# Token sums of the second and third seven-product group on GpSimd instead of VectorE

## The chip, the cores and the metric

One core of a Trainium2 chip runs the whole program in one launch. The metric is the device time of that launch in microseconds (us); lower is better. Engine names in the profile: PE is TensorE (PEld its weight loads), DVE is VectorE, ACT is ScalarE, POOL is GpSimd, SP is SyncE, which only issues transfers here.

## The reference

One decoder layer over 256 tokens of width 2048, all in float32: half a SwiGLU feed-forward, two token mixers side by side, half a second SwiGLU feed-forward, and a final norm.

```python
def rmsnorm(x, g):
    y = xf * lax.rsqrt(jnp.mean(xf * xf, axis=-1, keepdims=True) + NORM_EPS)
    return y * g

def swiglu(x, w_gate, w_up, w_down):
    return (jax.nn.silu(x @ w_gate) * (x @ w_up)) @ w_down

x = x + 0.5 * swiglu(rmsnorm(x, ffn1_norm), ffn1_w_gate, ffn1_w_up, ffn1_w_down)
... dilated attention and forgetting attention on rmsnorm(x, mix_norm) @ w_in, gated, projected, added ...
x = x + 0.5 * swiglu(rmsnorm(x, ffn2_norm), ffn2_w_gate, ffn2_w_up, ffn2_w_down)
return rmsnorm(x, final_norm)
```

D_MODEL is 2048 and D_FF is 5632. The change touches only the two feed-forwards.

## The kernel before

**Precision by splitting.** Each float32 operand of a product is split in two parts: ScalarE rounds it (`w_hi`, `xT_hi`, `pair_hi`), VectorE subtracts the rounded part from the original (`w_lo`, `xT_lo`, `pair_lo`), and TensorE adds three products, hi by hi, hi by lo and lo by hi (lines 551 to 553, 564 to 566). Weights come in slabs of two row tiles by 512 columns. A slab is loaded by SyncE, rounded by ScalarE, split by VectorE, and then used by TensorE. In a feed-forward six slab buffers are in rotation (four called `w_hi`/`w_lo`, two called `more_hi`/`more_lo`), so ScalarE and VectorE can be up to six slabs ahead of TensorE.

**A feed-forward.** D_FF is taken in 11 chunks of 512 columns. The first chunk is computed plainly: 16 slabs (8 of the gate weights, 8 of the up weights), 12 matmuls each. The other ten are "steps" of 33 slabs. Within a step, three of the four groups of row tiles are computed with seven products in place of eight, in Strassen's manner (`paired`). This needs sums of weights, made by VectorE for each step (`weight_sum`, lines 1329 to 1341, tile `sums`), and sums of tokens, made once for each feed-forward and each of the three groups: S1 to S4 in `pair_sums`, rounded by ScalarE into `pair_hi` and split by VectorE into `pair_lo`.

**Making the token sums.** `sum_pairs(f, g)` makes the four sums of group `g` of feed-forward `f` from the scaled, transposed tokens, which lie in `hidden` or `partial` (lines 1363 to 1366, 128 partitions by 256 elements each). S2 reads S1, and S4 reads S2. Then `round_pairs` on ScalarE (line 1006) and `split_pairs` on VectorE (line 1372) work on all four at once. There is one buffer `pair_sums`, so group `g` can be made only once group `g - 1` has been split (semaphore `s_lo`).

**Order around the change.** Every engine's order is written out by hand. During the first 16 slabs, with `o` the slab that TensorE is at, VectorE runs: split of slab `o + 6`, then at `o` = 3, 5, 7 `split_pairs` of groups 0, 1, 2, and at `o` = 4, 6 `sum_pairs` of groups 1, 2 (group 0 is made earlier). After `o` = 7 it takes the mean of squares (`take_mean`) and after `o` = 10 the reciprocal root (`take_rstd`), for which ScalarE's SiLU waits. ScalarE runs: rounding of slab `o + 6`, at `o` = 3, 5, 7 `round_pairs` of groups 0, 1, 2, and in the first feed-forward the squares of the tokens at `o` = 2 to 5. TensorE asks for the pair sums only at its first step (`pe.wait_ge(s_lo, (f + 1) * PAIRS)`). In the second feed-forward the tokens come out of the layer before, so group 0 is made at `o` = 1.

GpSimd has nothing to do in this stretch. It issues the 72 accumulating transfers `xres += gate_buf` (line 1301) in order, of which the first follows at the end of the first step.

Of the kernel before, what the change touches and what calls it, by code (L numbers as in the profile page):

```python
# [22 lines left out]
ALU = mybir.AluOpType  # L23
# [5 lines left out]
TT = SEQ // P  # L29
# [12 lines left out]
CH = 512  # L42
KT = D_MODEL // P
CT = CH // P
NN = D_MODEL // CH
# [11 lines left out]
STEPS = FF_CHUNKS - 1  # L57
# [17 lines left out]
PAIR_AT, PAIR_GROUPS, PAIR_SLABS = (0, 7, 18), (1, 2, 3), 7  # L75
PAIRS = len(PAIR_AT)
# [3 lines left out]
S1, S2, S3, S4 = 0, 1, 2, 3  # L80
# [84 lines left out]
def step_place(f, s, stride=0, i=None):  # L165

    return Place(FFN_START[f] + FIRST + s * STEP, FFN_LOAD[f] + FIRST_LOADS + s * STEP_LOADS,
                 stride * STEP, stride * STEP_LOADS, i)
# [6 lines left out]
def build(nc, x, ffn1_norm, ffn1_w_gate, ffn1_w_up, ffn1_w_down, mix_norm, w_in, b_forget,  # L175
# [15 lines left out]
    def sb(name, shape, dt=F32):  # L191
        return nc.alloc_sbuf_tensor(name, shape, dt)

    xres = sb("xres", [P, TT, D_MODEL])
# [32 lines left out]
    gate_buf = sb("gate_buf", [P, 2, TT, CH])  # L227
# [6 lines left out]
    pair_sums = nc.alloc_sbuf_tensor_at("pair_sums", [P, 4, 2, P], F32, offset=bias_at)  # L234
# [73 lines left out]
    def sem(name):  # L308
        return nc.alloc_semaphore(name)
# [11 lines left out]
    stored = sem("stored")  # L321
    summed = sem("summed")
    s_ready = sem("s_ready")
    s_hi = sem("s_hi")
    s_lo = sem("s_lo")
    m1_copied = sem("m1_copied")
    combined = sem("combined")
    down_copied = sem("down_copied")
    down_added = [sem(f"down_added{n}") for n in range(NN)]
# [6 lines left out]
    xt_scaled = sem("xt_scaled")  # L336
# [71 lines left out]
    with block:  # L408
# [115 lines left out]
        def scaled(n, t):  # L524
            return hidden[:, t] if n % 2 == 0 else partial[:, t]
# [8 lines left out]
        def tiles(ap):  # L534
            return ap.rearrange("p (k c) -> p k c", c=P)
# [434 lines left out]
        def _(act):  # L970
# [31 lines left out]

            def round_pairs(f, g):

                act.wait_ge(s_ready, PAIRS * f + g + 1)
                nc.scalar.activation(pair_hi[:, :, 2 * g:2 * g + 2], pair_sums[:, :, :, :],
                                     ACT.Copy).then_inc(s_hi, 1)

# [193 lines left out]
            with act.Fori(0, 2) as i:  # L1202
                place = mix_place(MIX, QKV_STEP, i)
                for part, banks in enumerate((A, B, C)):
                    for o in range(WIDE):
                        round_slab(place, part * WIDE + o + MIX_RING)
                        if part > 0 and o in (2, 4):
                            t = o // 2 - 1
# [26 lines left out]
            for c in range(6):  # L1235
                half, part = divmod(c, 3)
                for o in range(WIDE):
# [9 lines left out]
                    if part > 0 and o in (2, 4):  # L1247
                        t = o // 2 - 1
# [40 lines left out]
        @block.gpsimd  # L1289
        def _(pool):  # L1290
            pool.wait_ge(xt_hi, 2 * TT)
            pool.dma_start(tab[:, P:C_END], table[:, P:C_END]).then_inc(table_landed, 16)
            pool.dma_start(f_raw[:, :, :], in_w[:, :, F_COL:G_COL]).then_inc(forget_landed, 16)
            pool.dma_start(f_bias[:, :], b_forget.broadcast_to([P, HEADS])).then_inc(forget_landed, 16)
            pool.memset(f_abs[0:1, 0, 0:1], 0.0).then_inc(down_copied, 2)
            for j in range(2 * (STEPS - 1)):
                for n in range(NN):
                    pool.wait_ge(down_copied, j * NN + n + 3)
                    if j > 0:
                        pool.wait_ge(down_added[n], j * 16)  # L1300
                    pool.dma_start(xres[:, :, n * CH:(n + 1) * CH], gate_buf[:, n % 2],  # L1301
                                   accum_op=ALU.add).then_inc(down_added[n], 16)

        @block.vector
        def _(dve):
            chain = [0]

            def link(done):

                chain[0] += 1  # L1310
                done.then_inc(small, 1)
                dve.wait_ge(small, chain[0])

            def split_slab(place, offset):
                dve.wait_ge(hi_ready, place.slab(offset + 1))
                nc.vector.tensor_tensor(slot_lo(place, offset), raw_half(place, offset),  # L1316
                                        slot_hi(place, offset).bitcast(F32), ALU.subtract).then_inc(lo_ready, 1)

            def weight_sum(place, q, pair, which, count):

                at, base = PAIR_AT[pair], STEP * q
                up_l, gate_l = PAIR_LOADS[pair]
                up, gate = raw[:, up_l % LOADS], raw[:, gate_l % LOADS]
                done = count + SUMS_STEP * q + 4 * pair
                out = sums[:, SUM_PLACE[which]]
                if which == T3:
                    dve.wait_ge(lo_ready, place.slab(base + at - 2))
                    dve.wait_ge(raw_landed[up_l % LOADS], place.landed(STEP_LOADS * q + up_l))
                    made = nc.vector.tensor_tensor(out, up[:, 1::2, :], up[:, 0::2, :], ALU.subtract)
                if which == T1:  # L1330
                    dve.wait_ge(lo_ready, place.slab(base + at - 1))
                    dve.wait_ge(raw_landed[gate_l % LOADS], place.landed(STEP_LOADS * q + gate_l))
                    made = nc.vector.tensor_tensor(out, up[:, 0::2, :], gate[:, 0::2, :], ALU.subtract)
                if which == T2:
                    dve.wait_ge(lo_ready, place.slab(base + at + 1))
                    dve.wait_ge(summed, done + T3 + 1)
                    made = nc.vector.tensor_tensor(out, sums[:, SUM_PLACE[T3]], gate[:, 0::2, :], ALU.add)  # L1337
                if which == T4:
                    dve.wait_ge(lo_ready, place.slab(base + at + 3))
                    dve.wait_ge(summed, done + T2 + 1)  # L1340
                    made = nc.vector.tensor_tensor(out, gate[:, 1::2, :], sums[:, SUM_PLACE[T2]], ALU.subtract)
                made.then_inc(summed, 1)
# [14 lines left out]

            def sum_pairs(f, g):

                if g > 0:  # L1360
                    dve.wait_ge(s_lo, PAIRS * f + g)
                x0, x1 = (tiles(scaled(PAIR_GROUPS[g], t)) for t in range(TT))
                link(nc.vector.tensor_tensor(pair_sums[:, S1], x1[:, 0::2], x1[:, 1::2], ALU.add))
                nc.vector.tensor_tensor(pair_sums[:, S3], x0[:, 0::2], x1[:, 0::2], ALU.subtract)
                link(nc.vector.tensor_tensor(pair_sums[:, S2], pair_sums[:, S1], x0[:, 0::2], ALU.subtract))
                nc.vector.tensor_tensor(pair_sums[:, S4], x0[:, 1::2], pair_sums[:, S2],
                                        ALU.subtract).then_inc(s_ready, 1)
                dve.wait_ge(s_ready, PAIRS * f + g + 1)

            def split_pairs(f, g):  # L1370
                dve.wait_ge(s_hi, PAIRS * f + g + 1)
                nc.vector.tensor_tensor(pair_lo[:, :, 2 * g:2 * g + 2], pair_sums[:, :, :, :],
                                        pair_hi[:, :, 2 * g:2 * g + 2].bitcast(F32), ALU.subtract)\
                  .then_inc(s_lo, 1)
# [18 lines left out]
            def scale_x(b, n):  # L1393
                for t in range(TT):
                    scale_tokens(b, n, t)
                for t in range(TT):
                    split_x(b, n, t)
# [30 lines left out]
            def multiply_up(up, silu_count):  # L1428

                for t in range(TT):  # L1430
                    dve.wait_ge(silu_done, silu_count + t + 1)
                    nc.vector.scalar_tensor_tensor(hidden[:, t], up[t], rstd[:, t:t + 1],
                                                   chunk_buf[:, t], ALU.mult, ALU.mult)\
                      .then_inc(hidden_ready, 1)
# [32 lines left out]
            def ffn(f, b):  # L1467
                first = first_place(f)
                silu, count = f * FF_CHUNKS * TT, f * SUMS
                for o in range(FIRST):  # L1470
                    m = o + FFN_RING
                    if o == FIRST - 1:
                        dve.wait_ge(slab_done, first.slab(FIRST))
                        multiply_up([ps[:, FIRST_UP + t] for t in range(TT)], silu)
                    if m < FIRST:
                        if m == FIRST - 1:
                            weight_sum(step_place(f, 0), 0, 0, T3, count)
                        split_slab(first, m)
                    else:
                        split_step(step_place(f, 0), m - FIRST, count)  # L1480
                    if b > 0 and o == 1:
                        sum_pairs(f, 0)
                        scale_x(b, NN - 1)
                    if o in (3, 5, 7):
                        split_pairs(f, o // 2 - 1)
                    if o in (4, 6):
                        sum_pairs(f, o // 2 - 1)
                    if o == WIDE - 1:
                        take_mean(b)
                    if o == WIDE + 2:  # L1490
                        take_rstd(b)
# [128 lines left out]
            for o in (4, 5):  # L1620
                split_slab(first_place(0), o)
            sum_pairs(0, 0)
            scale_x(0, 3)
            ffn(0, 0)
# [169 lines left out]
```

## Time and profile before

| | |
|---|---|
| Median of 3 runs | 2069.49 us (2069.41 to 2069.68) |
| Profiled execution, its own time | 2069.33 us |
| Profiled execution, span of the trace | 2067.4 us |
| TensorE busy | 2053.4 us, 99% of the span |
| VectorE busy | 1680.3 us, 81% |
| ScalarE busy | 1206.9 us, 58% |
| GpSimd busy | 87.6 us, 4%, 80 instructions |
| Mean granted TensorE clock | 0.999 of full speed |

The span runs from the first to the last instruction; 1.93 us of the profiled execution's own time lie outside it. The first feed-forward begins at about 11 us, the second at about 1370 us of the span. A busy share is an average over all stages and says little about a stretch of 30 us; the stretches are read from the timeline. "Idle before" and the engine behind the arrow tell how long an engine stood before an instruction, and what it stood for.

### The profile page before, as it was taken

The numbers are of one execution on the slowest core, as the hardware profiler recorded it, in microseconds if no ns is written. First come the engines' busy times: TensorE is split into PE (matmuls) and PEld (weight loads), VectorE is DVE, ScalarE is ACT, GpSimd is POOL, SyncE is SP. The second block draws the span as 40 slices with busy tenths as digits, with TensorE's granted clock in tenths as the row PEclk, the third lists the DMA queues.
The fourth block names the chain that finished last, engine by engine and source line by source line (L and its number), as shares of the span: only waits on it lengthen the run. The fifth ranks groups of instructions, "written<-read, shape, count | busy, mean of one in ns | idle before, by whom it ended". The sixth has DMA issues, their size and how long they took to land.

```text
span 2067.4 us, 26644 instructions
## 1 busy us (share of the span) xinstructions
PE 2053.4 (99%) x9344; PEld 1702.8 (82%) x9344; DVE 1680.3 (81%) x1703; ACT 1206.9 (58%) x1394; POOL 87.6 (4%) x80
## 2 busy tenths in 40 slices
PE   9999999999999999999999999999999999999998
PEld 7788888888888888888888888888888888888886
DVE  7999999999999744555455655689999999999997
ACT  6666666666666444554544344466666666666664
POOL 0000000000000000000000000000000000000000
PEclk9999999999999999999999999999999999999999
DMA  8578777778877455545445665555877777887773
GB/s 280 204 220 256 231 236 247 233 217 250 238 234 242 141 195 186 183 163 174 162 156 197 198 202 194 184 185 181 251 237 232 246 231 224 244 243 231 246 232 126
DMA packets 222139, 441.01 MB, mean 213 GB/s; under 512 B 7648, under 2 KB 7824, under 8 KB 221936
## 3 DMA queue, kind: packets, MB, share of 16 engines
q1 hardware_dynamic: 202112, 401.64, 56.1%
q0 software_dynamic: 19744, 38.28, 11.2%
q8 instruction: 48, 0.79, 0.2%
q14 instruction: 27, 0.22, 0.0%
q10 hardware_dynamic: 208, 0.08, 0.0%
HBM read 400.13 MB, written 2.10 MB: 195 GB/s over the span
## 4 chain that ended last, share of the span: by engine, by line
PE 96%; DVE 2%; ACT 1%; issue 1%; DMA 0%; SPq 0%; ACTq 0%; DVEq 0%
PE ps L551 20%; PE ps L553 20%; PE ps L552 20%; PE ps L564 9%; PE ps L566 9%; PE ps L565 9%; PE ps L761 2%; PE ps L763 2%; PE ps L762 2%; PE ps L616 1%; DVE w_lo L1316 0%; DVE w_lo L1355 0%; DMA raw<-in_ffn_w_gate 0%; PE ps L772 0%; PE ps L597 0%
## 5 line engine op out<-in xcount | busy, mean ns | idle before, releaser
L1316 DVE TENSOR_TENSOR w_lo<-raw,w_hi 128x1024 fp32r<-128x1024 f32 x256 | 312.9, 1225 | 287.8 <-ACT w_hi L988 287.6
L988 ACT ACTIVATE w_hi<-raw 128x1024 fp32r<-128x1024 f32 x256 | 269.9, 1058 | 305.7 <-PE ps L553 301.0
L1355 DVE TENSOR_TENSOR w_lo<-raw,w_hi 128x1024 fp32r<-128x1024 f32 x280 | 338.0, 1219 | 7.2 <-ACT w_hi L1001 5.1
L551 PE MATMUL ps<-w_hi,xT_hi 128*128 128x512 f32 x856 | 340.0, 397 | 0.4 <-DVE xT_lo L1390 0.4
L553 PE MATMUL ps<-w_hi,xT_lo 128*128 128x512 f32 x856 | 334.1, 390 | 0.0
L552 PE MATMUL ps<-w_lo,xT_hi 128*128 128x512 f32 x856 | 333.6, 390 | 0.0
L1001 ACT ACTIVATE w_hi<-raw 128x1024 fp32r<-128x1024 f32 x280 | 290.8, 1053 | 72.5 <-PE ps L553 53.8
L1001 ACT ACTIVATE w_hi<-sums 128x1024 fp32r<-128x1024 f32 x160 | 169.8, 1063 | 203.7 <-PE ps L553 71.4
L1355 DVE TENSOR_TENSOR w_lo<-sums,w_hi 128x1024 fp32r<-128x1024 f32 x160 | 195.2, 1222 | 34.0 <-ACT w_hi L1001 31.4
L551 PE MATMUL ps<-w_hi,hT_hi 128*128 128x512 f32 x536 | 208.9, 390 | 0.0
L553 PE MATMUL ps<-w_hi,hT_lo 128*128 128x512 f32 x536 | 208.7, 389 | 0.0
L552 PE MATMUL ps<-w_lo,hT_hi 128*128 128x512 f32 x536 | 208.7, 389 | 0.0
L553 PEld LDWEIGHTS ps<-w_hi,xT_lo 128*128 128x128 f32 x856 | 160.7, 188 | 34.3
L551 PEld LDWEIGHTS ps<-w_hi,xT_hi 128*128 128x128 f32 x856 | 161.0, 188 | 32.2 <-DVE xT_lo L1390 0.6
L552 PEld LDWEIGHTS ps<-w_lo,xT_hi 128*128 128x128 f32 x856 | 161.0, 188 | 31.8
L1355 DVE TENSOR_TENSOR more_lo<-raw,more_hi 128x1024 fp32r<-128x1024 f32 x140 | 169.2, 1219 | 6.6 <-ACT more_hi L1001 5.6
L1001 ACT ACTIVATE more_hi<-raw 128x1024 fp32r<-128x1024 f32 x140 | 146.4, 1053 | 33.3 <-PE ps L553 23.7
L1301 POOL DMA_DIRECT2D xres<-gate_buf x72 | 84.9, 1179 | 1875.6 <-ACT gate_buf L1122 1830.6
L1001 ACT ACTIVATE more_hi<-sums 128x1024 fp32r<-128x1024 f32 x80 | 85.0, 1063 | 99.7 <-DVE sums L1337 24.1
L564 PE MATMUL ps<-w_hi,pair_hi 128*128 128x512 f32 x300 | 117.0, 390 | 1.0 <-DVE w_lo L1355 1.0
L553 PEld LDWEIGHTS ps<-w_hi,hT_lo 128*128 128x128 f32 x536 | 100.6, 188 | 20.9
L551 PEld LDWEIGHTS ps<-w_hi,hT_hi 128*128 128x128 f32 x536 | 100.7, 188 | 20.8
(251 smaller groups left out, 3840.8 us busy)
## 6 DMA issues: line engine op xcount, KB each, us to landing
raw<-in_ffn_w_up SPq DMA_DIRECT2D x88, 1024.0 KB, 5.4
raw<-in_ffn_w_down SPq DMA_DIRECT2D x88, 1024.0 KB, 5.3
raw<-in_ffn_w_gate SPq DMA_DIRECT2D x87, 1024.0 KB, 5.4
raw<-in_w_in SPq DMA_DIRECT2D x80, 1024.0 KB, 5.0
xres<-gate_buf POOLq DMA_DIRECT2D x72, 512.0 KB, 5.5
raw<-in_w_out SPq DMA_DIRECT2D x16, 1024.0 KB, 5.1
raw<-in_w_proj_dil SPq DMA_DIRECT2D x8, 1024.0 KB, 5.1
raw<-in_w_proj_fox SPq DMA_DIRECT2D x8, 1024.0 KB, 5.1
```

Source lines behind the costliest of these rows:

```text
L551: nc.tensor.matmul(acc, hi, hi_w[:, j], start=first and j == 0, stop=False)
L552: nc.tensor.matmul(acc, hi, lo_w[:, j], start=False, stop=False)
L553: done = nc.tensor.matmul(acc, lo, hi_w[:, j], start=False, stop=last and j == 1)
L564: nc.tensor.matmul(acc, hi, hi_w[:, j], start=first and j == 0, stop=False)
L565: nc.tensor.matmul(acc, hi, lo_w[:, j], start=False, stop=False)
L566: done = nc.tensor.matmul(acc, lo, hi_w[:, j], start=False, stop=last and j == 1)
L761: nc.tensor.matmul(acc, hi, hi_w[:, j], start=begin, stop=False)
L988: nc.scalar.activation(slot_hi(place, offset), raw_half(place, offset), ACT.Copy).then_inc(hi_ready, 1)
L1001: nc.scalar.activation(slot_hi(place, offset), src, ACT.Copy).then_inc(hi_ready, 1)
L1301: pool.dma_start(xres[:, :, n * CH:(n + 1) * CH], gate_buf[:, n % 2], accum_op=ALU.add).then_inc(down_added[n], 16)
L1316: nc.vector.tensor_tensor(slot_lo(place, offset), raw_half(place, offset), slot_hi(place, offset).bitcast(F32), ALU.subtract).then_inc(lo_ ...
L1355: nc.vector.tensor_tensor(slot_lo(place, offset), step_source(r)[0], slot_hi(place, offset).bitcast(F32), ALU.subtract).then_inc(lo_ready, 1)
```

## The change

For groups 1 and 2 of both feed-forwards, the four sums are made by GpSimd. VectorE keeps group 0. GpSimd waits for the scaled tokens and for the split of the group before, and counts its own sums in a new semaphore `pair_summed`; ScalarE's `round_pairs` waits for `s_ready_pool` in place of `s_ready` in these groups. The transfers of GpSimd keep their order; the sums of each feed-forward stand ahead of that feed-forward's transfers.

```diff
             def round_pairs(f, g):
 
-                act.wait_ge(s_ready, PAIRS * f + g + 1)
+                if g == 0:
+                    act.wait_ge(s_ready, f + 1)
+                else:
+                    act.wait_ge(s_ready_pool, (PAIRS - 1) * f + g)
...
+            def sum_pairs(f, g):
+
+                pool.wait_ge(xt_scaled, (f * 2 * NN + PAIR_GROUPS[g] + 1) * TT)
+                pool.wait_ge(s_lo, PAIRS * f + g)
+                x0, x1 = (tiles(scaled(PAIR_GROUPS[g], t)) for t in range(TT))
+                done = (f * (PAIRS - 1) + g - 1) * 3
+                nc.gpsimd.tensor_tensor(pair_sums[:, S1], x1[:, 0::2], x1[:, 1::2], ALU.add)\
+                  .then_inc(pair_summed, 1)
+                nc.gpsimd.tensor_tensor(pair_sums[:, S3], x0[:, 0::2], x1[:, 0::2], ALU.subtract)\
+                  .then_inc(pair_summed, 1)
+                pool.wait_ge(pair_summed, done + 2)
+                nc.gpsimd.tensor_tensor(pair_sums[:, S2], pair_sums[:, S1], x0[:, 0::2], ALU.subtract)\
+                  .then_inc(pair_summed, 1)
+                pool.wait_ge(pair_summed, done + 3)
+                nc.gpsimd.tensor_tensor(pair_sums[:, S4], x0[:, 1::2], pair_sums[:, S2],
+                                        ALU.subtract).then_inc(s_ready_pool, 1)
+
+            for f in range(2):
+                for g in range(1, PAIRS):
+                    sum_pairs(f, g)
+                for j in range(f * (STEPS - 1), (f + 1) * (STEPS - 1)):
...
             def sum_pairs(f, g):
 
-                if g > 0:
-                    dve.wait_ge(s_lo, PAIRS * f + g)
...
-                dve.wait_ge(s_ready, PAIRS * f + g + 1)
+                dve.wait_ge(s_ready, f + 1)
...
                     if o in (3, 5, 7):
                         split_pairs(f, o // 2 - 1)
-                    if o in (4, 6):
-                        sum_pairs(f, o // 2 - 1)
```

## Rows read from the trace of the kernel before

**Rows 1.** The page, busy time of each engine (share of the span) and instructions.
```profile
PE 2053.4 (99%) x9344; PEld 1702.8 (82%) x9344; DVE 1680.3 (81%) x1703; ACT 1206.9 (58%) x1394; POOL 87.6 (4%) x80
```
**Rows 2.** The page, the chain that ended last, by engine.
```profile
PE 96%; DVE 2%; ACT 1%; issue 1%; DMA 0%; SPq 0%; ACTq 0%; DVEq 0%
```
**Rows 3.** Waits of TensorE over the span: total us, times, longest.
```profile
PE ps L564 <- DVE w_lo L1355: 1.5, 3, 0.6
```
**Rows 4.** Windows: length, then busy us (x instructions) of PE, PEld, DVE, ACT, POOL.
```profile
45.00:62.00 17.00, 17.00 (x77) 14.09 (x76) 16.58 (x23) 12.48 (x14) 0.00 (x0) 1.00 0.41 130
62.00:80.00 18.00, 16.53 (x73) 12.40 (x72) 18.00 (x17) 11.92 (x13) 0.00 (x0) 1.00 0.57 196
...
1400.00:1434.00 34.00, 34.00 (x154) 28.11 (x153) 33.23 (x39) 21.81 (x24) 0.00 (x0) 1.00 0.50 162
```
**Rows 5.** Timeline of TensorE, first step: start, duration, what, idle before.
```profile
67.42 0.39 PE L565 MATMUL ps<-more_lo,pair_hi 128*128 128x512 f32 x1
67.64 0.39 PE L566 MATMUL ps<-more_hi,pair_lo 128*128 128x512 f32 x1
68.46 0.50 PE L564 MATMUL ps<-w_hi,xT_hi 128*128 128x512 f32 x1 [0.43 <-DVE w_lo L1355]
68.80 0.40 PE L565 MATMUL ps<-w_lo,xT_hi 128*128 128x512 f32 x1
...
70.73 0.50 PE L564 MATMUL ps<-w_hi,pair_hi 128*128 128x512 f32 x1 [0.62 <-DVE w_lo L1355]
...
74.21 0.50 PE L564 MATMUL ps<-w_hi,pair_hi 128*128 128x512 f32 x1 [0.43 <-DVE w_lo L1355]
```
**Rows 6.** Instructions on tile `pair_sums`: count, ns min/median/max, first and last start.
```profile
L1366 DVE TENSOR_TENSOR pair_sums<-partial,pair_sums x4: 424/424/425, 24.1 to 1397.2; 128x256 f32<-128x256 f32 x4
```
**Rows 7.** Timeline of VectorE, first feed-forward.
```profile
32.67 1.22 DVE L1372 TENSOR_TENSOR pair_lo<-pair_sums,pair_hi 128x1024 fp32r<-128x1024 f32 x1
...
37.50 1.23 DVE L1316 TENSOR_TENSOR more_lo<-raw,more_hi 128x1024 fp32r<-128x1024 f32 x1
38.64 1.22 DVE L1372 TENSOR_TENSOR pair_lo<-pair_sums,pair_hi 128x1024 fp32r<-128x1024 f32 x1
...
44.77 1.22 DVE L1372 TENSOR_TENSOR pair_lo<-pair_sums,pair_hi 128x1024 fp32r<-128x1024 f32 x1
```
**Rows 8.** Timeline of ScalarE, first feed-forward.
```profile
35.75 1.05 ACT L988 ACTIVATE more_hi<-raw 128x1024 fp32r<-128x1024 f32 x1
37.50 1.06 ACT L1006 ACTIVATE pair_hi<-pair_sums 128x1024 fp32r<-128x1024 f32 x1 [0.70 <-DVE pair_sums L1366]
...
39.69 2.00 ACT L988 ACTIVATE w_hi<-raw 128x1024 fp32r<-128x1024 f32 x2
43.62 1.06 ACT L1006 ACTIVATE pair_hi<-pair_sums 128x1024 fp32r<-128x1024 f32 x1 [1.93 <-DVE pair_sums L1366]
...
46.60 1.28 ACT L1030 ACT_TABLE_LOAD   x1
```
**Rows 9.** Timeline of VectorE, second feed-forward.
```profile
1388.55 1.22 DVE L1372 TENSOR_TENSOR pair_lo<-pair_sums,pair_hi 128x1024 fp32r<-128x1024 f32 x1
...
1393.67 1.22 DVE L1372 TENSOR_TENSOR pair_lo<-pair_sums,pair_hi 128x1024 fp32r<-128x1024 f32 x1
...
1414.60 1.41 DVE L1432 SCALAR_TENSOR_TENSOR hidden<-ps,rstd,chunk_buf 128x512 f32<-128x512 f32 x2 [0.34 <-PE ps L553]
...
1430.40 1.22 DVE L1355 TENSOR_TENSOR more_lo<-raw,more_hi 128x1024 fp32r<-128x1024 f32 x1
```
**Rows 10.** Timeline of ScalarE, second feed-forward.
```profile
1392.53 1.06 ACT L1006 ACTIVATE pair_hi<-pair_sums 128x1024 fp32r<-128x1024 f32 x1 [2.50 <-DVE pair_sums L1366]
...
1397.64 1.06 ACT L1006 ACTIVATE pair_hi<-pair_sums 128x1024 fp32r<-128x1024 f32 x1 [2.16 <-DVE pair_sums L1366]
```
**Rows 11.** Timeline of TensorE, second feed-forward, first step.
```profile
1432.55 0.39 PE L564 MATMUL ps<-more_hi,xT_hi 128*128 128x512 f32 x1
```
**Rows 12.** The page, costliest groups: busy us, mean ns of one, idle before.
```profile
L1301 POOL DMA_DIRECT2D xres<-gate_buf x72 | 84.9, 1179 | 1875.6 <-ACT gate_buf L1122 1830.6
```

More of the change, by code:

```diff
@@ L323, in build @@
     s_ready = sem("s_ready")
+    s_ready_pool = sem("s_ready_pool")
+    pair_summed = sem("pair_summed")
     s_hi = sem("s_hi")
@@ L1295, in _ @@
             pool.memset(f_abs[0:1, 0, 0:1], 0.0).then_inc(down_copied, 2)
[L1296 to L1302, printed above, removed]
+            def sum_pairs(f, g):
[17 more added lines that the diff above has]
+                for j in range(f * (STEPS - 1), (f + 1) * (STEPS - 1)):
+                    for n in range(NN):
+                        pool.wait_ge(down_copied, j * NN + n + 3)
+                        if j > 0:
+                            pool.wait_ge(down_added[n], j * 16)
+                        pool.dma_start(xres[:, :, n * CH:(n + 1) * CH], gate_buf[:, n % 2],
+                                       accum_op=ALU.add).then_inc(down_added[n], 16)
         @block.vector
```

## The prediction

> **What bounds the kernel.** I read the page first: TensorE is busy 99% of the span and VectorE 81% [rows 1], and TensorE makes up 96% of the chain that ended last [rows 2]. So work taken off VectorE is worth nothing unless TensorE waits for VectorE at that place. The waits of TensorE over the whole span show one such kind once the kernel is under way: three stops for the split weights, 1.5 us together [rows 3]. The timeline has them at 68.46, 70.73 and 74.21 us, in the first step of the first feed-forward [rows 5]. What such a stop costs is more than its idle mark: matmuls follow each other at 0.22 us (67.42 to 67.64), but 67.64 to 68.46 is 0.82, so 0.60 is lost, and the next follows at 0.34, 0.12 more: 0.7 us for a mark of 0.43. With the same 0.28 on top of each mark, the three cost 1.5 + 3 x 0.28 = 2.3 us. That is all that this change could win, since TensorE has no stop for VectorE in the second feed-forward: it is busy all 34.0 us of 1400 to 1434 [rows 4].
>
> The windows say why the stops are there. VectorE is busy 16.58 of 17 us in 45 to 62 and 18.00 of 18 in 62 to 80 [rows 4]. It works without a pause up to the point where TensorE catches up with it. So whatever time VectorE has lost or won by about 46 us arrives at 68 to 74 us nearly whole: a loss makes each stop longer, a win shortens them until the 2.3 us are used up. In the second feed-forward there is a cushion. VectorE stood 0.34 us for TensorE at 1414.60, and the closest place after that is the split that ends at 1430.40 + 1.22 = 1431.62, which TensorE takes up at 1432.55: 0.93 us to spare [rows 9, 11]. A delay there costs what exceeds 0.34 + 0.93 = 1.27 us.
>
> **What is taken away.** Four groups of four sums leave VectorE, 16 instructions of 0.42 us [rows 6], 6.8 us of its busy time. For the end only one thing counts: when `pair_lo` of the last group is done, since ScalarE and VectorE run in order, and behind it stand the mean, the reciprocal root, SiLU and all slabs.
>
> **What is put in: a longer loop.** ScalarE was already standing for these sums: 0.70 and 1.93 us in the first feed-forward [rows 8], 2.50 and 2.16 in the second [rows 10]. That is the loop that matters: split of group g - 1, sums of group g, rounding, split of group g. Call S the time from the end of one `pair_lo` to the start of the next `pair_hi`, now GpSimd's to fill.
>
> First feed-forward. `pair_lo` of group 0 ends at 32.67 + 1.22 = 33.89 [rows 7]. `pair_hi` of group 1 can start at 33.89 + S, and not before ScalarE has finished its slab: it stood 0.70 before 37.50, so from 36.80 [rows 8]. From the start of a `pair_hi` to the end of its `pair_lo` it is 38.64 + 1.22 - 37.50 = 2.36 [rows 7, 8]. So `pair_hi` of group 2 starts at 33.89 + 2.36 + 2S = 36.25 + 2S, where it now starts at 43.62 [rows 8]. The delay is 2S - 7.37 us: even at S = 3.69. If S is small, ScalarE's other work holds it: it was free again at 43.62 - 1.93 = 41.69, 4.19 after the `pair_hi` before, so 36.80 + 4.19 = 41.0 is the earliest, 2.6 us before now.
>
> Second feed-forward. `pair_lo` of group 0 ends at 1388.55 + 1.22 = 1389.77, `pair_hi` to `pair_lo` is again 1393.67 + 1.22 - 1392.53 = 2.36 [rows 9, 10], so group 2 is rounded from 1392.13 + 2S, now 1397.64: a delay of 2S - 5.51, of which 1.27 is covered.
>
> When S is over 3.69, TensorE ends later by (2S - 7.37) + (2S - 5.51 - 1.27) = 4S - 14.15 us. Everything hangs on S, four times over.
>
> **How large is S.** No row shows arithmetic of any size on GpSimd. Below, a sum can hardly be quicker than VectorE's own 0.42 us [rows 6]; above, I take the only sizable instruction of GpSimd in the trace, the issue of a transfer, 1.18 us [rows 12]. The sum has VectorE's shape and type, so I go nearer to that row: 0.6 us, an estimate. There are two handovers inside the group (S2 waits for S1, S4 for S2) and one each side, together an estimated 0.2. Alone on its data, GpSimd then has S = 4 x 0.6 + 0.2 = 2.6.
>
> It is not alone. While it sums, VectorE has two slab splits to do in each group, and a split takes 1.14 us from start to start (37.50 to 38.64) [rows 7]. Each such split reads two tiles in SBUF, as each sum does. If the two engines must take turns, S is 2.6 + 2 x 1.14 = 4.88, because both splits have their weights rounded in time and get in between the sums; GpSimd's first and second sum come before the first split only where VectorE happens to wait for ScalarE. If they don't disturb each other, S stays 2.6. No row of this trace shows both engines at arithmetic, so both remain open; I take turns as the likelier.
>
> The Trainium skill (SBUF — State Buffer, section Who interferes with whom) speaks for that and against this change: a VectorE instruction with two SBUF inputs contends with a GpSimd instruction that reads SBUF, since its second input comes over GpSimd's read interface, and the loser waits for the whole instruction. No row here shows it. The skill (GPSIMD Engine Reference, Reconciling with measured numbers) also gives 4497 ns against 2293 for a sum of 2048 elements; at that ratio of 1.96, 0.42 becomes 0.82 and S would be 3.5 without turns and 5.8 with them, 9 us on the whole time by the last.
>
> **The sum.** With S = 4.88 the first feed-forward gives 2 x 4.88 - 7.37 = 2.4 us, the second 2 x 4.88 - 5.51 - 1.27 = 3.0, together +5.4. The profiled execution's own time is 2069.33, so it becomes 2074.7; its median of three is 0.16 above it, and I forecast 2074.9 us.
>
> Edits that I cost at nothing. TensorE's own wait for all `pair_lo` stands after the 16 plain slabs; the last one is done at 44.77 + 1.22 = 46.0 [rows 7], and TensorE goes through 45 to 62 with 17.00 of 17 us busy [rows 4], with the first pair matmuls in its second half. GpSimd's transfers wait for ScalarE's `gate_buf`, 1830.6 us of its 1875.6 idle us [rows 12], and the first of each feed-forward comes at the end of a step; the sums are done before the first step, so they delay no transfer. SyncE's loads wait for splits and shift with them. The two new semaphores cost a few waits on an idle queue. What is queued behind the waiting `round_pairs` is ScalarE's next slabs, and VectorE waits for those; that is inside the loop above.
>
> **Rivals.**
> - No turns: the sums and splits overlap, S = 2.6. Then ScalarE's own work sets the first group (36.80), group 2 is rounded at 36.80 + 2.36 + 2.6 = 41.8 in place of 43.62, 1.9 us earlier, and the stops shrink by that. The second feed-forward's delay is below zero. Time 2067.6. For it: VectorE and GpSimd are separate engines, and nothing in the trace shows them in each other's way. It decides below S = 3.69; up to about 3.3 the whole stays under 2069.
> - One turn in each group, or no turns and a sum of 0.85 to 1.0 us: S = 3.7 to 4.4, so 4S - 14.15 is +0.7 to +3.5, about 2071.5.
> - Sums as slow as the 1.18 us row with both turns: S = 4 x 1.18 + 0.2 + 2.28 = 7.2, +14.7 us, 2084. Also here: the first arithmetic on GpSimd costs extra once, as ScalarE's table load does (1.28 us [rows 8]), which would be paid once in the first feed-forward on top of the forecast, 2076.2. The rest of this case lies around 2080.
> - The change doesn't do what it says: excluded in the code, except that VectorE's time is freed where it would otherwise be waiting for ScalarE, which is what the loop accounts for.
>
> **How the numbers follow.** Chances: turns (S about 4.5 to 5.6) 0.46; the middle case 0.23; no turns 0.23; slower than forecast by far 0.08. About 0.2%, 4.1 us, is what a measurement of this kernel can tell from no change. A gain is capped at 2.3 us, so faster by more than that bound gets 0.02, for the case that I misjudge the cap. The bound on the other side is passed at 4S - 14.15 = 4.1, S = 4.57: nearly all of the turns case and all of the slow one, 0.50. The rest is 0.48. The range reaches from the no-turns case with a quick sum, 2067.2, to S = 5.8, 2078.5. The forecast case's own range is 2073.3 to 2077.5.
>
> **What will show it.** Right: POOL with 16 instructions more, VectorE with 16 fewer and some 6.8 us less busy; ScalarE's wait before `pair_hi` now for GpSimd, some 2 and 3 us in the first feed-forward and over 4 in the second; `pair_hi` of group 2 at about 46 and 1401.9; TensorE's stops around 68 to 74 longer by 2.4 us, and new ones around 1425 to 1435. GpSimd's four sums spread over about 4.9 us with splits of VectorE between them. Wrong in size if the sums start 0.6 us apart although splits run beside them, or if splits that run beside a sum get longer than 1.22 us. Wrong in kind if TensorE's stops have gone, or if the chain runs through a transfer.

## The result and the profile after

The changed kernel takes 2075.47 us (median of 8 runs, 2075.21 to 2075.85) against 2069.47 us of the kernel before (2069.26 to 2069.68): 6.0 us more, ratio 1.0029, 95% interval 1.0018 to 1.0040. The median lies 0.29% above, more than the 0.2% that can be told from no change; the interval stays above 1 but begins just under that mark, at 1.0018. Forecast were 2074.9 us, in a range of 2067.2 to 2078.5.

The page of the changed kernel, the line that answers to [rows 1]:

```profile
PE 2057.0 (99%) x9344; PEld 1703.1 (82%) x9344; DVE 1676.7 (81%) x1687; ACT 1206.2 (58%) x1394; POOL 107.2 (5%) x96
```

GpSimd has 16 instructions more, VectorE 16 fewer. But VectorE is only 3.6 us less busy, where the 16 sums were 6.8 us of its time. The rest came back as longer splits, as the timelines show: time in which VectorE waits inside an instruction counts as busy.

What TensorE waited for, in two windows of the changed kernel (50 to 90 us, then 1400 to 1450; total us, times, longest), against [rows 3]:

```profile
PE ps L566 <- DVE w_lo L1381: 2.3, 5, 0.6
PE ps L566 <- DVE more_lo L1381: 0.6, 1, 0.6
...
PE ps L566 <- DVE w_lo L1381: 1.6, 3, 0.6
PE ps L566 <- DVE more_lo L1381: 0.3, 1, 0.3
```

Three stops of 1.5 us have become six of 2.9 us in the first feed-forward, and there are four new ones, 1.9 us, in the second, which had none. These are idle marks; at the prediction's price of 0.28 us on top of each mark, the first feed-forward's stops grew from 2.3 to 4.6 us.

GpSimd in the changed kernel, timeline, first feed-forward and then second:

```profile
34.28 0.73 POOL L1308 TENSOR_TENSOR pair_sums<-hidden 128x256 f32<-128x256 f32 x1 [16.95 <-DVE pair_lo L1396]
34.98 1.72 POOL L1310 TENSOR_TENSOR pair_sums<-hidden 128x256 f32<-128x256 f32 x1
36.78 0.73 POOL L1313 TENSOR_TENSOR pair_sums<-pair_sums,hidden 128x256 f32<-128x256 f32 x1
37.59 1.60 POOL L1316 TENSOR_TENSOR pair_sums<-hidden,pair_sums 128x256 f32<-128x256 f32 x1
...
1392.83 1.57 POOL L1308 TENSOR_TENSOR pair_sums<-hidden 128x256 f32<-128x256 f32 x1 [767.62 <-DVE pair_lo L1396]
1394.38 1.71 POOL L1310 TENSOR_TENSOR pair_sums<-hidden 128x256 f32<-128x256 f32 x1
1396.16 0.74 POOL L1313 TENSOR_TENSOR pair_sums<-pair_sums,hidden 128x256 f32<-128x256 f32 x1
1396.98 0.74 POOL L1316 TENSOR_TENSOR pair_sums<-hidden,pair_sums 128x256 f32<-128x256 f32 x1
```

Two of the four sums of each group take 0.73 us and two take 1.6 to 1.7. VectorE at the same time, same kernel:

```profile
32.90 1.22 DVE L1396 TENSOR_TENSOR pair_lo<-pair_sums,pair_hi 128x1024 fp32r<-128x1024 f32 x1
34.88 1.23 DVE L1342 TENSOR_TENSOR more_lo<-raw,more_hi 128x1024 fp32r<-128x1024 f32 x1 [0.76 <-ACT more_hi L990]
37.06 1.53 DVE L1342 TENSOR_TENSOR more_lo<-raw,more_hi 128x1024 fp32r<-128x1024 f32 x1 [0.95 <-ACT more_hi L990]
40.32 1.23 DVE L1396 TENSOR_TENSOR pair_lo<-pair_sums,pair_hi 128x1024 fp32r<-128x1024 f32 x1 [1.73 <-ACT pair_hi L1011]
42.50 3.39 DVE L1342 TENSOR_TENSOR w_lo<-raw,w_hi 128x1024 fp32r<-128x1024 f32 x2 [0.95 <-ACT w_hi L990]
47.61 1.23 DVE L1396 TENSOR_TENSOR pair_lo<-pair_sums,pair_hi 128x1024 fp32r<-128x1024 f32 x1 [1.72 <-ACT pair_hi L1011]
...
1391.45 1.22 DVE L1396 TENSOR_TENSOR pair_lo<-pair_sums,pair_hi 128x1024 fp32r<-128x1024 f32 x1
1392.59 2.90 DVE L1342 TENSOR_TENSOR more_lo<-raw,more_hi 128x1024 fp32r<-128x1024 f32 x2
1398.84 1.23 DVE L1396 TENSOR_TENSOR pair_lo<-pair_sums,pair_hi 128x1024 fp32r<-128x1024 f32 x1 [3.35 <-ACT pair_hi L1011]
```

The long second sum (34.98 to 36.70) lies beside the split of 34.88 to 36.11, which began 0.1 us before it and lasts its usual 1.23. The split of 37.06 begins inside the third sum: now the sum keeps its 0.73 us and the split lasts 1.53, not 1.22, and the fourth sum then waits for it. In each of these meetings the instruction that began first kept its length, and the later one was longer. The two splits of 42.50 take 3.39 us, where two undisturbed ones take 2.36. And VectorE, whose time was to be spared, now stands before `pair_lo`, 1.73 and 3.35 us.

ScalarE in the changed kernel, the rows that answer to [rows 8, 10]:

```profile
39.23 1.06 ACT L1011 ACTIVATE pair_hi<-pair_sums 128x1024 fp32r<-128x1024 f32 x1 [2.20 <-POOL pair_sums L1316]
...
46.52 1.06 ACT L1011 ACTIVATE pair_hi<-pair_sums 128x1024 fp32r<-128x1024 f32 x1 [3.10 <-POOL pair_sums L1316]
...
1397.75 1.06 ACT L1011 ACTIVATE pair_hi<-pair_sums 128x1024 fp32r<-128x1024 f32 x1 [4.81 <-POOL pair_sums L1316]
...
1405.13 1.06 ACT L1011 ACTIVATE pair_hi<-pair_sums 128x1024 fp32r<-128x1024 f32 x1 [4.42 <-POOL pair_sums L1316]
```

From these rows and VectorE's `pair_lo` (the first ends at 32.90 + 1.22 = 34.12) S, the time from the end of a `pair_lo` to the next `pair_hi`, can be read: 39.23 - 34.12 = 5.11, 46.52 - 41.55 = 4.97, 1397.75 - 1392.67 = 5.08 and 1405.13 - 1400.07 = 5.06 us, together 20.22. The prediction's sum, 4S - 14.15, with these four in place of 4S, is then 20.22 - 14.15 = 6.07 us; 6.00 were measured.

### The profile page after: what moved, and what is told of

Same layout as the page of the kernel before. It is cut to its first block, busy times and chain, and to the rows that moved or that the text cites. A ratio compares the mean times of both kernels' runs of the same rounds, so it can differ in the third digit from the quotient of the medians.

```text
span 2073.6 us, 26646 instructions
## 1 busy us (share of the span) xinstructions
PE 2057.0 (99%) x9344; PEld 1703.1 (82%) x9344; DVE 1676.7 (81%) x1687; ACT 1206.2 (58%) x1394; POOL 107.2 (5%) x96
## 4 chain that ended last, share of the span: by engine, by line
PE 95%; DVE 2%; ACT 1%; issue 1%; POOL 0%; DMA 0%; SPq 0%; DVEq 0%; ACTq 0%; POOLq 0%
PE ps L553 20%; PE ps L555 20%; PE ps L554 20%; PE ps L566 9%; PE ps L568 9%; PE ps L567 9%; PE ps L765 2%; PE ps L763 2%; PE ps L764 2%; PE ps L618 1%; DVE w_lo L1381 1%; DMA raw<-in_ffn_w_gate 0%; PE ps L774 0%; PE ps L599 0%; PE ps L831 0%
## 5 line engine op out<-in xcount | busy, mean ns | idle before, releaser
L554 PEld LDWEIGHTS ps<-w_lo,hT_hi 128*128 128x128 f32 x536 | 100.6, 188 | 20.7
```

Of the source, the lines that this page charges most:

```text
L554: nc.tensor.matmul(acc, hi, lo_w[:, j], start=False, stop=False)
```

## The experiments

Each time below is a median beside runs of the kernel before on the same chip (2069.34 to 2069.44 us).

**One feed-forward at a time.** Groups 1 and 2 go to GpSimd only for `f == MOVED`; the other keeps VectorE's sums.

```diff
-                for g in range(1, PAIRS):
+                for g in range(1, PAIRS if f == MOVED else 1):
                     sum_pairs(f, g)
...
+                    if o in (4, 6) and f != MOVED:
+                        sum_pairs(f, o // 2 - 1)
```

Expected with `MOVED = 0`:

> Only the first feed-forward's two groups go to GpSimd; the second keeps VectorE's sums. Loop theory (the delay is the sum of the two S of a feed-forward less what the loop takes now): S of 5.11 and 4.97 us as in the changed kernel, 10.08 - 7.37 = +2.7 us over the kernel before, 2072.2. Rival (a cost paid once, at the first arithmetic on GpSimd or at the start): nearly all of the 6.0 us is here, 2075.

Expected with `MOVED = 1`:

> Only the second feed-forward's two groups go to GpSimd. Loop theory: 5.08 + 5.06 - 5.51 - 1.27 = +3.4 us over the kernel before, 2072.8, with TensorE's stops of the first feed-forward back at 1.5 us of marks and new ones near 1425 to 1436. Rival (a cost paid once): +0, or the full 6.

Measured: 2072.14 us with the first (ratio 1.0013, 1.0004 to 1.0022), 2072.72 us with the second (1.0016, 1.0007 to 1.0025). That is +2.7 and +3.3, against 2.7 and 3.4 expected, and together the 6.0 of the whole change. So the rival of a cost paid once, which expected nearly all of it in one half, falls. It also shows the cushion: the second feed-forward is delayed more than the first (its loop was shorter before, 2S - 5.51 against 2S - 7.37): 5.08 + 5.06 - 5.51 = 4.63 us of delay cost 3.3, so 1.3 us were covered, where the prediction had 1.27.

**Splits kept out of the sums' way.** The changed kernel, with VectorE held before its two splits.

```diff
+                    if o in (4, 6):
+                        dve.wait_ge(s_ready_pool, (PAIRS - 1) * f + o // 2 - 1)
                     if m < FIRST:
```

> The changed kernel, but VectorE starts the two slab splits of each group only when GpSimd's four sums are done, so nothing of VectorE's runs beside them. Theory of turns: every sum takes 0.73 us, S falls from 5.05 to about 3.25, and the splits run beside ScalarE's rounding; the loop of a group goes from 7.4 to 6.8 us, 1.2 us less in each feed-forward: 2073.0. Rival (GpSimd's slow sums have another cause): the 1.6 us sums stay, S stays at 5.05, and 2 x 1.14 us of splits come on top in part: 2080 or more.

Measured: 2073.16 us (1.0018, 1.0009 to 1.0027), 2.3 us below the changed kernel although VectorE is held back (2073.0 were expected). Instructions of GpSimd on `pair_sums` in this kernel (count, ns min/median/max):

```profile
L1308 POOL TENSOR_TENSOR pair_sums<-hidden x2: 731/734/736, 34.0 to 1391.5; 128x256 f32<-128x256 f32 x2
L1310 POOL TENSOR_TENSOR pair_sums<-hidden x2: 725/727/729, 34.7 to 1392.2; 128x256 f32<-128x256 f32 x2
L1313 POOL TENSOR_TENSOR pair_sums<-pair_sums,hidden x2: 741/741/741, 35.5 to 1393.0; 128x256 f32<-128x256 f32 x2
L1316 POOL TENSOR_TENSOR pair_sums<-hidden,pair_sums x2: 735/736/736, 36.3 to 1393.8; 128x256 f32<-128x256 f32 x2
```

These are group 1 of both feed-forwards; group 2's sums take 735 to 742 ns. No long sum is left, and no long split: VectorE is busy 1673.6 us in this kernel, 6.7 less than before, so nearly all of the 6.8 us now shows. S is 3.25 us in each group. Waiting on purpose was cheaper than colliding, since the splits now lie beside ScalarE's rounding. VectorE stands 3.25 us in each group, 13.0 in all, hardly more than the 12.8 us that it stands in the changed kernel for its splits and `pair_lo`.

**One sum more.**

```diff
+                nc.gpsimd.tensor_tensor(spare[:, :, :], x1[:, 0::2], x1[:, 1::2], ALU.add)\
+                  .then_inc(pair_summed, 1)
                 nc.gpsimd.tensor_tensor(pair_sums[:, S1], x1[:, 0::2], x1[:, 1::2], ALU.add)\
```

> The changed kernel with a fifth sum on GpSimd ahead of the four of each group, of the same shape, into a spare tile: S is longer by one undisturbed sum, 0.70 to 0.80 us, in each of four groups. Loop theory (TensorE's end moves by the sum of the four S): +2.8 to +3.2 us over the changed kernel, 2078.5. Rival (the cost is in the turns alone, and GpSimd's own time is hidden): no change, 2075.5. If the fifth sum lost a turn of its own: 2080.

Measured: 2078.21 us (1.0042, 1.0029 to 1.0056), 2.74 us above the changed kernel, just under the expected 2.8 to 3.2, and 0.69 for each of the four extra sums, which start 0.70 us before the next. So GpSimd's time in these four places arrives whole at the end of the kernel; it isn't the turns alone that cost.

**The two engines side by side, without the layer.** Eight sums 128x256 on GpSimd, started together with five instructions 128x1024 of another engine (this kernel computes nothing of the layer; the code is shortened).

```python
for i in range(8):
    nc.gpsimd.tensor_tensor(sum_out[:, c, i], a[:, 0::2], a[:, 1::2], ALU.add)
# beside it, for c = 1, 2, 3 on VectorE and c = 4 on ScalarE, five times:
nc.vector.tensor_tensor(o, xin[:, 1, 0:1024], xin[:, 1, 1024:2048], ALU.subtract)
nc.vector.tensor_tensor(o, flat, xin[:, 1, 0:1024], ALU.subtract)     # flat is in PSUM
nc.vector.tensor_scalar(o, xin[:, 1, 0:1024], 2.0, None, ALU.mult)
nc.scalar.activation(wide_out[:, 4, i], xin[:, 1, 0:1024], ACT.Copy)
```

> Not the layer: five stretches of eight GpSimd sums 128x256, each beside five instructions 128x1024 of another engine: nothing; VectorE subtract with both inputs in SBUF; VectorE subtract with one input in PSUM; VectorE tensor_scalar from SBUF; ScalarE copy. The output is x, not the layer. Theory of turns over a shared way for the second input: sums 0.7 us alone and beside the PSUM form and ScalarE; beside the form with two SBUF inputs the eight sums take 5.6 + up to 5 x 1.14 us. Rival (any VectorE work, or any use of SBUF, slows GpSimd): the PSUM form or ScalarE slow it as well.

Windows of this kernel: length, then busy us (x instructions) of DVE, ACT and POOL. The first is GpSimd with nothing beside it but VectorE's one copy from SBUF into PSUM, the others follow the list above.

```profile
8.35:13.93 5.58, 1.18 (x1) 0.00 (x0) 5.50 (x9) 1.00 0.00 0
13.93:24.38 10.45, 8.42 (x5) 0.00 (x0) 10.38 (x8) 1.00 0.00 0
24.38:30.27 5.89, 5.75 (x5) 0.00 (x0) 5.50 (x8) 1.00 0.00 0
30.28:36.00 5.72, 5.21 (x5) 0.00 (x0) 5.69 (x5) 1.00 0.00 0
38.10:44.30 6.20, 0.00 (x0) 6.11 (x6) 5.50 (x9) 1.00 0.00 0
```

VectorE's two forms of subtraction, groups by line (mean ns of one behind the busy us):

```profile
L68 DVE TENSOR_TENSOR wide_out<-xin 128x1024 f32<-128x1024 f32 x5 | 8.4, 1746 | 4.4 <-POOL sum_out L52 4.4
L70 DVE TENSOR_TENSOR wide_out<-ps,xin 128x1024 f32<-128x1024 f32 x5 | 5.7, 1215 | 2.0 <-POOL sum_out L52 2.0
```

The start of the stretch with two SBUF inputs, GpSimd's first two sums and VectorE's first subtraction, and the `tensor_scalar` (count, ns min/median/max):

```profile
13.91 0.72 POOL L52 TENSOR_TENSOR sum_out<-xin 128x256 f32<-128x256 f32 x1
14.59 1.71 POOL L52 TENSOR_TENSOR sum_out<-xin 128x256 f32<-128x256 f32 x1
13.94 1.77 DVE L68 TENSOR_TENSOR wide_out<-xin 128x1024 f32<-128x1024 f32 x1 [4.41 <-POOL sum_out L52]
...
L72 DVE TENSOR_SCALAR wide_out<-xin x5: 695/1207/1214, 30.3 to 34.3; 128x1024 f32<-128x1024 f32 x5
```

Eight sums take 5.5 us alone, and 5.5 beside the subtraction that has one input in PSUM or beside ScalarE. Beside the subtraction with both inputs in SBUF they take 10.4 (up to 11.3 were expected), and that subtraction takes 1746 ns in place of the 1.22 us of an undisturbed split in the layer: both engines lose. The first rows show how. GpSimd's first sum began 0.03 us before the subtraction and took its usual 0.72; the subtraction stood for it (1.77), the next sum stood for the subtraction (1.71), and so on, one for one. From 13.94 to the last start at 20.6 a subtraction begins every 1.67 us, where one of each alone takes 1.14 + 0.68 = 1.82 from start to start: turns, with some 0.15 us of overlap. The `tensor_scalar` is in the same turns though it reads one tensor: the first, which began before GpSimd's sum, took 695 ns, the other four about 1207, and only about five sums fit into 5.7 us. The expectation's theory of the second input doesn't cover that form, and no run here shows its reason. So it isn't any use of SBUF that gets in the way, as the rival had it, but the kind of VectorE instruction.

**Buffers of their own, sums as early as possible.** The sums of groups 1 and 2 lie in `gate_buf`, idle at that time, and GpSimd no longer waits for the split of the group before.

```diff
+    more_sums = [nc.alloc_sbuf_tensor_at(f"more_sums{g}", [P, 4, 2, P], F32,
+                                         offset=gate_at + g * 2 * CH * 4) for g in range(PAIRS - 1)]
...
                 pool.wait_ge(xt_scaled, (f * 2 * NN + PAIR_GROUPS[g] + 1) * TT)
-                pool.wait_ge(s_lo, PAIRS * f + g)
+                if f == 1:
+                    pool.wait_ge(slab_done, FFN2)
+                out = sums_of(g)
```

> The changed kernel, but groups 1 and 2 have buffers of their own for the sums (in a tile that is idle then), so GpSimd needs no split of the group before and sums as soon as the scaled tokens are there. Loop theory: S leaves the loop, ScalarE never stands for a sum, VectorE is 2 to 3 us earlier at the first step and TensorE's stops vanish: 2.3 us less than the kernel before, 2067.2. Rival (sums on GpSimd slow VectorE's splits by turns wherever they are): VectorE loses as much as it is spared, 2069.5; or the change costs by itself, 2072 and more.

Measured: 2072.28 us (1.0011, 1.0002 to 1.0020; the runs spread from 2070.69 to 2072.88). The expectation of 2067.2 missed. Its first part held: no stop is left in either first step. But the turns now lie where the tokens are still being prepared. Timelines of this kernel, GpSimd, VectorE, TensorE:

```profile
18.92 0.74 POOL L1315 TENSOR_TENSOR more_sums<-hidden 128x256 f32<-128x256 f32 x1 [1.87 <-DVE hidden L1414]
...
18.93 2.42 DVE L1421 TENSOR_TENSOR xT_lo<-hidden,xT_hi 128x512 fp32r<-128x512 f32 x2
21.28 3.43 DVE L1349 TENSOR_TENSOR more_lo<-raw,more_hi 128x1024 fp32r<-128x1024 f32 x2
...
29.09 0.39 PE L560 MATMUL ps<-more_hi,xT_lo 128*128 128x512 f32 x1
31.95 0.47 PE L558 MATMUL ps<-w_hi,xT_hi 128*128 128x512 f32 x1 [2.47 <-DVE w_lo L1349]
...
32.96 0.63 PE L558 MATMUL ps<-w_hi,xT_hi 128*128 128x512 f32 x1
33.39 0.63 PE L559 MATMUL ps<-w_lo,xT_hi 128*128 128x512 f32 x1
```

The token split takes 2.42 us where the pairs of its kind without a neighbour take 1.29, the two weight splits 3.43, and TensorE, which has nearly nothing in hand here, stands from 29.09 to 31.95: 2.86 us between starts, 2.6 more than the usual 0.22. Then matmuls follow at 0.43 us. The granted clock says why, in the windows 28 to 32 and 32 to 36 of this kernel (the number after the busy times):

```profile
28.00:32.00 4.00, 1.53 (x8) 0.98 (x6) 4.00 (x4) 4.00 (x7) 3.84 (x4) 1.00 0.59 219
32.00:36.00 4.00, 4.00 (x11) 3.15 (x12) 4.00 (x4) 4.00 (x9) 0.39 (x1) 0.57 0.30 69
```

0.57 over this stretch means that TensorE, which had stood for 2.5 us and ran at 1.00 before, was granted mostly the lower of its two levels (1.2 of 2.4 GHz) after the stop. It did 11 matmuls in 4 us; the kernel before did 19 there, at a granted clock of 1.00. At 0.22 us each, that is another 1.8 us. With 0.5 us for a stop at 1390.03 (0.77 between starts) the bill is 2.6 + 1.8 + 0.5 - 2.3 for the stops gone = +2.6, measured +2.9; the 0.3 left over are not accounted for.

**The same, started later.** GpSimd waits in addition for the last token split, and in the first feed-forward for eight weight slabs; then a version of this in the first feed-forward alone.

```diff
-                pool.wait_ge(xt_scaled, (f * 2 * NN + PAIR_GROUPS[g] + 1) * TT)
+                pool.wait_ge(xt_lo, (f * 2 + 1) * NN * TT)
+                if f == 0:
+                    pool.wait_ge(lo_ready, WIDE)
```

> As own_buffers (sums of groups 1 and 2 in tiles of their own, no wait for the split of the group before), but GpSimd starts only after the last token split of the feed-forward, and in the first one only after eight weight slabs are split, at about 30 us. Theory: what own_buffers lost was turns at 19 to 31 us, ahead of the last token tile, where TensorE has almost nothing in hand; started later, the turns fall where VectorE leads TensorE by over a slab and waits for ScalarE now and then, and neither S nor the early stop remains: 2067.2 to 2068.5, the stops of the first step gone or small. Rival (each sum on GpSimd costs VectorE about as much as doing it itself, whatever the place): 2069.4.

> The same only in the first feed-forward; the second keeps VectorE's sums as in the kernel before. Theory: only the first has stops to win, so the time equals own_late within 0.3 us. If own_late is slower than this one, the second feed-forward still pays for GpSimd there.

Measured: 2068.17 us (2068.01 to 2068.26; ratio 0.9994, 0.9985 to 1.0003) and 2068.14 us. The interval of the first reaches above 1, though no run of this kernel is as slow as the fastest of the kernel before (2069.26). The early stop has gone, and of the stops of the first step two are left, at 69.6 and 73.1 us, 0.47 and 0.86 between starts. All eight sums of the first feed-forward run from 30.12 to 42.48, seven of them at 1.6 to 1.7 us, in turns with splits that grow to 1.75 to 1.80. The last `pair_lo` begins at 43.60, 1.2 us earlier than in the kernel before (44.77 [rows 7]), and 1.24 us are won. So even at the best place found GpSimd gives only part of the 2.3 us. The second feed-forward costs nothing any more: moved or not, the time is the same within 0.03 us.

**The same tiles, VectorE's sums.** No GpSimd: the kernel before with `more_sums`, and the sums of groups 1 and 2 two slabs earlier.

```diff
-                    if o in (4, 6):
-                        sum_pairs(f, o // 2 - 1)
+                    if o in (2, 4):
+                        sum_pairs(f, o // 2)
```

> The kernel before (all sums on VectorE), with sums of groups 1 and 2 in tiles of their own and made two slabs earlier, so that ScalarE need not stand for them. It tells what of own_late's gain is GpSimd's and what the separate tiles'. If the tiles are what matters: VectorE fills with the sums the 0.6 to 0.9 us gaps in which it waits for ScalarE (0.58, 0.76 and 0.91 us between 31 and 41), and the time is 2067.4 to 2068.5, as good as own_late or better. If VectorE's spared work is what matters, the time is that of the kernel before, 2069.4.

Measured: 2066.92 us (2066.82 to 2067.15), ratio 0.9988, 0.9979 to 0.9997: 2.4 us below the kernel before, below the 2067.4 to 2068.5 that were expected, and the fastest of all. VectorE in this kernel:

```profile
27.37 3.50 DVE L1321 TENSOR_TENSOR w_lo<-raw,w_hi 128x1024 fp32r<-128x1024 f32 x3 [0.25 <-ACT w_hi L993]
30.78 0.42 DVE L1367 TENSOR_TENSOR more_sums<-hidden 128x256 f32<-128x256 f32 x1
...
42.16 1.22 DVE L1376 TENSOR_TENSOR pair_lo<-more_sums,pair_hi 128x1024 fp32r<-128x1024 f32 x1
```

From 27.37 on it has no idle time up to the last `pair_lo`, which begins at 42.16, not 44.77 [rows 7]: 2.6 us earlier with the same work. TensorE has no stop left in the first step. The 2.4 us are the whole 2.3 that the prediction gave as the most to be won. This gain is below 0.2%, but its runs and those of the kernel before don't overlap.

## Why the prediction was right

**What bounds the kernel.** Right. Three stops worth 2.3 us were all that a faster VectorE could win; the last experiment won 2.4 and left no stop. The cushion of 1.27 us in the second feed-forward is borne out by the two halves, 2.7 and 3.3 us.

**The loop.** Right, and the part that carries the result. S in place of VectorE's busy time decided: 16 instructions left VectorE, and the kernel got slower. The extra sum showed the slope (0.69 us for each sum in each group). Separate tiles showed that without the loop the loss of the changed kernel does not arise: the same sums on GpSimd gave 2068.2 where they were placed late. Placed as early as possible they lost 2.9 us, but in another way, mostly at 29 to 36 us, ahead of the first step, which had no stop.

**The size of S.** 4.88 forecast, 5.06 on average. Two terms were off, in opposite ways. A sum takes 0.73 us, not 0.6, with starts 0.70 apart, so S without turns is not 2.6 but the 3.25 of the splits-after kernel: its sums start 0.15 us after the split and run 3.06 us in all. The turns cost 5.06 - 3.25 = 1.8 us in a group, not 2.28; a split and a sum overlap in part. That 0.65 too little and 0.47 too much nearly cancelled is luck: with the sums right and the turns as forecast, S would have been 5.53 and the time 2077.5, 2 us above what was measured. By the ratio that the prediction took from the Trainium skill (GPSIMD Engine Reference, Reconciling with measured numbers) a sum would be an estimated 0.82; the runs say 0.73.

**Turns.** Right in kind, and shown: by the splits-after kernel and by the side-by-side one. The rule of the Trainium skill (SBUF — State Buffer, Who interferes with whom) agrees with the runs in what contends: two SBUF inputs yes (10.4 us for eight sums), one input in PSUM no (5.5), ScalarE no (5.5). It has the one that starts first keep its way and the other stand until that instruction is over, and the rows bear this out within the overlap of 0.15 us: the first sum (0.72), the first `tensor_scalar` (695 ns) and the split of 34.88 (1.23) kept their length, and what began beside them was longer. That VectorE's subtraction is at 1746 ns in the mean is no exception, since each of the five began while a sum was running.

**The rivals.** No turns (2067.6) failed on the long sums. The first arithmetic on GpSimd cost nothing extra: its first sum took 0.73 us, and each feed-forward paid its own share. VectorE's splits grew too, so that only 3.6 us of its 6.8 show as saved. The prediction had counted the turns as GpSimd's loss alone, and splits longer than 1.22 us were among the signs of being wrong in size; that sign came (1.53 us at 37.06). It cost little beyond what S counts, since behind these splits VectorE stands for `pair_hi` anyway.

**The signs named.** `pair_hi` of group 2 in the first feed-forward was forecast at 46, came at 46.5; in the second at 1401.9, came at 1405.1, of which 2.7 are the first feed-forward's delay. The rest is the larger S and 0.2 us by which the trace of the changed kernel is already later at `pair_lo` of group 0 (34.12 against 33.89). ScalarE's waits were forecast as 2 and 3, then over 4 twice, and are 2.20, 3.10, 4.81 and 4.42. TensorE's stops in the first step grew by 2.3 us at the prediction's price, against 2.4 forecast, and the new ones came at 1426.4 to 1435.7.

## What to carry to other kernels

Before moving work to an idle engine, look for the loop it closes: here the sums stood between two splits because of one shared buffer, and each microsecond added to one group's sums came back four times, once for each group moved, while the saved time of the busy engine counted for nothing. Break the loop first (another buffer, an earlier place in the order); here that alone gave all there was to win, on the engine that had the work already. And GpSimd is no free neighbour of a VectorE that subtracts two tiles in SBUF, or scales one into another: cost both as slower wherever they overlap, and keep them apart where the engine they feed has nothing in hand.

## What the runs showed of the hardware

A GpSimd sum of 128x256 float32 takes 0.73 us against VectorE's 0.42, at 0.70 us from start to start. Beside 128x1024 VectorE subtractions with two SBUF inputs the two engines take turns: what begins second stands, so that sums take 1.6 to 1.7 us and subtractions grow from 1.22 to about 1.75, and a pair of one each takes 1.67 us. A `tensor_scalar` of 128x1024 from SBUF to SBUF takes such turns too, 0.70 us when it begins first and 1.21 when it doesn't. Beside a subtraction with one PSUM input, or a copy on ScalarE, nothing changes. In one case, a stop of TensorE of 2.9 us between starts was followed by 4 us at a granted clock of 0.57, which cost 1.8 us on top of the stop's 2.6; stops of up to 1.0 us between starts, as in the first steps, left the granted clock at 1.00.
